# A hybrid decoder step on one core: TensorE's narrow matmuls, once grouped by head or by sampled token, taken in turn between column groups

## The reference, cut to what matters

```python
# stick-breaking attention, 8 heads of 64, prompt tokens among themselves
out = einsum("bhij,bjhd->bihd", weights, v)          # "value products" of the prompt
# the same for each sampled token over its 512 cached positions (4 pages of 128)
out = einsum("bhij,bjhd->bihd", weights, v_all)      # "value products" of the sampled tokens
# SSD (Mamba-2), 16 heads of 64, state 128, chunks of 128 tokens
y_diag = einsum("bclsg,bclsge,bcsgep->bclgep", cb, decay, xd)
y_off  = einsum("bclgn,bcgepn,bclge->bclgep", cc, h_in, exp(cs))
y = y_diag + y_off
```

## Time and profile before

| | |
|---|---|
| median of 3 runs | 1539.03 us (1538.46 to 1540.69) |
| profiled execution, span from first to last instruction | 1537.4 us (no other time is listed for it; 1.6 us lie between it and the median) |
| TensorE matmuls busy | 1486.9 us, 97% of the span |
| VectorE busy | 829.3 us, 54% |
| ScalarE busy | 496.8 us, 32% |
| GpSimd busy | 208.4 us, 14% |
| mean granted TensorE clock | 0.989 |
| attention turns | about 397 to 666 us |
| sampled tokens' values with their gate units | 773 to 849 us |
| SSD tiles | about 854 to 1002 us |

### The profile page before, as it was taken

How to read it: one execution, slowest core, us unless ns; L and a number is a source line. 1 busy time by engine, 2 the same in 40 slices (tenths; PEclk the granted TensorE clock), 3 DMA queues, 4 the chain that set the end, 5 groups by cost and what they waited for, 6 DMA issues and landing times.

```text
span 1537.4 us, 28766 instructions
## 1 busy us (share of the span) xinstructions
PE 1486.9 (97%) x11698; PEld 1425.1 (93%) x11698; DVE 829.3 (54%) x973; ACT 496.8 (32%) x715; POOL 208.4 (14%) x159
## 2 busy tenths in 40 slices
PE   5999999999999999996999998999999999999999
PEld 5999999999999898986976887889999999999999
DVE  6444444333364745676865699967554444443222
ACT  4222222222252433521222555454323222222121
POOL 4000000010000000033500567711020000000000
PEclk9999999999999999997999999999999999999999
DMA  5323323334331321354944835365523323323322
GB/s 154 97 82 95 95 83 92 97 102 121 96 90 55 89 82 55 95 201 142 318 142 130 124 112 157 77 183 172 165 82 97 95 82 95 95 83 89 100 89 79
DMA packets 279480, 172.56 MB, mean 112 GB/s; under 512 B 13344, under 2 KB 261376, under 8 KB 279296
## 3 DMA queue, kind: packets, MB, share of 16 engines
q1 hardware_dynamic: 273120, 156.80, 36.1%
q0 software_dynamic: 2848, 8.60, 1.7%
q10 hardware_dynamic: 3456, 6.39, 1.1%
HBM read 154.04 MB, written 17.73 MB: 112 GB/s over the span
## 4 chain that ended last, share of the span: by engine, by line
PE 86%; DVE 10%; DMA 2%; issue 1%; ACT 1%; SPq 1%; POOL 0%; DVEq 0%; ACTq 0%
PE ps L426 75%; PE ps L1802 3%; PE ps L1703 2%; DVE w_lo L407 2%; DVE gbuf L1260 2%; PE ps L1593 1%; PE ps L1619 1%; DVE bt L1101 1%; PE ps L1603 1%; DVE prod L1295 1%; PE ps L1609 1%; DMA out_ssd_p<-hin 1%; DVE hin L1253 1%; DVE ydec L1271 1%; PE ps L1583 0%
## 5 line engine op out<-in xcount | busy, mean ns | idle before, releaser
L426 PE MATMUL ps<-xg_hi,w_hi 128*128 128x260 f32 x2512 | 519.4, 288 | 37.2 <-DVE w_lo L407 32.0
L426 PE MATMUL ps<-xg_hi,w_lo 128*128 128x260 f32 x2512 | 510.7, 285 | 0.0
L426 PE MATMUL ps<-xg_lo,w_hi 128*128 128x260 f32 x2512 | 510.3, 285 | 0.0
L426 PEld LDWEIGHTS ps<-xg_hi,w_hi 128*128 128x128 f32 x2512 | 392.7, 191 | 49.7 <-issue 24.7
L407 DVE TENSOR_TENSOR w_lo<-stage,w_hi 128x1024 fp32r<-128x1024 f32 (+1 forms) x229 | 296.5, 1295 | 243.0 <-ACT w_hi L402 237.7
L426 PEld LDWEIGHTS ps<-xg_hi,w_lo 128*128 128x128 f32 x2512 | 392.2, 191 | 0.0
L426 PEld LDWEIGHTS ps<-xg_lo,w_hi 128*128 128x128 f32 x2512 | 391.6, 191 | 0.0
L402 ACT ACTIVATE w_hi<-stage 128x1024 fp32r<-128x1024 f32 (+1 forms) x229 | 237.1, 1035 | 316.2 <-PE ps L426 248.0
L426 PE MATMUL ps<-hid_hi,w_hi 128*128 128x260 f32 x704 | 141.9, 283 | 0.0
L426 PE MATMUL ps<-hid_hi,w_lo 128*128 128x260 f32 x704 | 141.5, 282 | 0.0
L426 PE MATMUL ps<-hid_lo,w_hi 128*128 128x260 f32 x704 | 141.3, 282 | 0.0
(11 more groups left out here) (282 smaller groups left out, 1598.5 us busy)
## 6 DMA issues: line engine op xcount, KB each, us to landing
stage<-in_w_in SPq DMA_DIRECT2D x69, 512.0 KB, 4.9
stage<-in_ffn_w_gate SPq DMA_DIRECT2D x44, 512.0 KB, 3.8
stage<-in_ffn_w_up SPq DMA_DIRECT2D x44, 512.0 KB, 3.9
stage<-in_ffn_w_down SPq DMA_DIRECT2D x32, 448.0 KB, 3.5
stage<-in_ffn_w_down SPq DMA_DIRECT2D x16, 512.0 KB, 3.7
pages<-in_cache_sb_k SPq DMA_DIRECT2D x32, 256.0 KB, 4.1
pages<-in_cache_sb_v SPq DMA_DIRECT2D x32, 256.0 KB, 3.2
gates<-gates_kept POOLq DMA_DIRECT2D x24, 260.0 KB, 3.6
```

The costliest lines, as they stand in the source:

```text
L426: mm = nc.tensor.matmul(out[:, h, :], wt[:, r, k, :], v[:, h * HALF:(h + 1) * HALF], start=start and k == 0 and n == 0, stop=stop and k == ...
```

## The change

In all three places the matmuls that write different rows of one PSUM bank, and so use different column groups of TensorE's array, are issued in turn. In attention both heads' value products stand together at the end of the turn. In the sampled part the four gate units of a turn come first and then the 16 matmuls of its four slots, page by page. In the SSD part `turn(t + 1)` moves ahead of both heads' products, `spread(t + 1, 0)` behind them, and the products wait for both heads' inputs; `turn` waits for ScalarE's two reads of bank 4 (`seg_ready`, `ecs_ready`) in place of the products made from them.

```diff
-                def values(e):
-                    pe.wait_ge(w_ready.sem, w_ready.now(t, e))
+                def values():
                     pe.wait_ge(v_tok_ready.sem, v_tok_ready.now(t))
-                    cols = slice(HD * e, HD * e + HD)
+                    pe.wait_ge(w_ready.sem, w_ready.now(t, 1))
                     for j in range(CH):
-                        mm = nc.tensor.matmul(ps[cols, 7, P * j:NP], v_tok[:, j, cols], ...
-                    mm.then_inc(pv_done.sem, 1)
+                        for e in range(2):
+                            cols = slice(HD * e, HD * e + HD)
+                            mm = nc.tensor.matmul(ps[cols, 7, P * j:NP], v_tok[:, j, cols], ...
+                            if j == CH - 1:
+                                mm.then_inc(pv_done.sem, 1)
...
                 unit(6)
-                values(0)
                 unit(7, end=2)
                 tails(1)
                 unit(7, begin=2)
-                values(1)
+                values()
...
                 for b in range(SLOTS):
                     gate(G0_V + b, SLOTS * i)
+                pe.wait_ge(wd4_ready.sem, wd4_ready.now(i))
+                for b in range(SLOTS):
                     pe.wait_ge(page_landed[b], 64 * i + 64 * (NS // SLOTS + 1))
-                    pe.wait_ge(wd4_ready.sem, wd4_ready.now(i))
-                    rows = slice(4 * SB_HEADS * b, 4 * SB_HEADS * (b + 1))
-                    for g in range(PAGES):
+                for g in range(PAGES):
+                    for b in range(SLOTS):
+                        rows = slice(4 * SB_HEADS * b, 4 * SB_HEADS * (b + 1))
                         mm = nc.tensor.matmul(ps[rows, 7, :], wd4[:, g, :],
                                               pages[:, b, g, :], start=g == 0, stop=g == PAGES - 1)
-                    mm.then_inc(pvd_done.sem, 1)
+                        if g == PAGES - 1:
+                            mm.then_inc(pvd_done.sem, 1)
...
             def turn(t):
                 pe.wait_ge(xs_ready.sem, xs_ready.now(t // SLOTS, t % SLOTS))
                 if t:
-                    pe.wait_ge(g_ready.sem, g_ready.now(0, 2 * t - 1))
-                    pe.wait_ge(csc_ready.sem, csc_ready.now(0, 2 * t - 1))
+                    pe.wait_ge(seg_ready.sem, seg_ready.now(0, 2 * t - 1))
+                    pe.wait_ge(ecs_ready.sem, ecs_ready.now(0, 2 * t - 1))
...
+                if t < SSD_T - 1:
+                    turn(t + 1)
                 for e in range(2):
                     pe.wait_ge(g_ready.sem, g_ready.now(0, 2 * t + e))
                     pe.wait_ge(csc_ready.sem, csc_ready.now(0, 2 * t + e))
-                    if e == 0:
-                        pe.wait_ge(hin_ready.sem, hin_ready.now(0, t))
-                        pe.wait_ge(y_ready.sem, y_ready.now(0, t - 1))
-                    rows = slice(HD * e, HD * e + HD)
-                    for c in range(CH):
-                        cols = slice(P * c, P * c + P)
+                pe.wait_ge(hin_ready.sem, hin_ready.now(0, t))
+                pe.wait_ge(y_ready.sem, y_ready.now(0, t - 1))
+                for c in range(CH):
+                    cols = slice(P * c, P * c + P)
+                    for e in range(2):
+                        rows = slice(HD * e, HD * e + HD)
                         nc.tensor.matmul(ps[rows, 7, cols], xd[:, t % 2, c, rows], gbuf[:, e, cols], start=True, stop=False)
+                    for e in range(2):
+                        rows = slice(HD * e, HD * e + HD)
                         mm = nc.tensor.matmul(ps[rows, 7, cols], hin[:, c, rows], csc[:, e, cols], start=False,
                                               stop=True)
-                    if e == 0 and t < SSD_T - 1:
-                        turn(t + 1)
-                        spread(t + 1, 0)
                 mm.then_inc(y_summed.sem, 1)
+                if t < SSD_T - 1:
+                    spread(t + 1, 0)
```

More of the change, by code:

```diff
@@ L1612, in tails @@
                     mm.then_inc(tail_summed.sem, 1)
-                def values(e):
-                    pe.wait_ge(w_ready.sem, w_ready.now(t, e))
+                def values():
                     pe.wait_ge(v_tok_ready.sem, v_tok_ready.now(t))
-                    cols = slice(HD * e, HD * e + HD)
+                    pe.wait_ge(w_ready.sem, w_ready.now(t, 1))
                     for j in range(CH):
-                        mm = nc.tensor.matmul(ps[cols, 7, P * j:NP], v_tok[:, j, cols],
-                                              zb[:, e, SCORE_AT[j]:SCORE_AT[j] + SCORE_W[j]],
-                                              start=j == 0, stop=j == CH - 1)
-                    mm.then_inc(pv_done.sem, 1)
+                        for e in range(2):
+                            cols = slice(HD * e, HD * e + HD)
+                            mm = nc.tensor.matmul(ps[cols, 7, P * j:NP], v_tok[:, j, cols],
+                                                  zb[:, e, SCORE_AT[j]:SCORE_AT[j] + SCORE_W[j]],
+                                                  start=j == 0, stop=j == CH - 1)
+                            if j == CH - 1:
+                                mm.then_inc(pv_done.sem, 1)
                 unit(0)
```

## The result

The changed kernel takes 1524.31 us (median of 4 runs, 1523.8 to 1526.46); the kernel before, beside it, 1538.74. The ratio is 0.9904, with a 95% interval of 0.9892 to 0.9916. By the medians that is 14.4 us less, by the ratio 14.8, where 12.9 had been forecast (1526 us; range 1519 to 1536). The profiled execution spans 1524.7 us, 12.7 less than the one before; it is the slowest of the four (1526.46 us), so its trace shows some 2 us less of the gain than the median does.

What follows compares the result with a forecast made beforehand. TensorE was taken to bound attention and the sampled part, VectorE the SSD tiles. The terms -6.4 - 7.1 + 0.6 = -12.9 us, from 1539.0, gave 1526 us, range 1519 to 1536.

Steps and rivals of the forecast that it cites:

- Two column groups run together: Narrow matmuls of two column groups, as in the last SSD tile, run at twice the rate of one.
- Four groups: Sampled tokens' value products: four column groups assumed to run all at once, 2 x 3.43 us for two blocks.
- rival of two streams: Sampled part: only two column groups overlap, L1703 at 7 us a block, gain there only -1.6 us.
- A, attention, -6.4 us: Four attention turns, both heads' value products merged: 2.25 us saved less 0.65 waited, 1.6 us per turn.
- B, sampled tokens, -7.1 us: Sampled part, two turns: 68.9 us against 76.0 with four streams, including a new wait and a lower clock.
- wait for the gate weights: Sampled part: TensorE stands 12.8 us, once, for gate weights queued behind SyncE's wait and sixteen page loads.
- lower clock: Sampled part: after the idle time TensorE resumes at granted clock 0.50, losing 2.4 us (bounds 0 and 3).
- C, SSD, +0.6 us: Eight SSD tiles: VectorE sets the pace, TensorE's savings become idle time; bounds -2 and +3 us.
- absorption of tile 0's 1.8 us by the store of `hin`: SSD tile 0: VectorE's 1.80 us wait for the output turns into a longer wait for the store of `hin`.
- dips of the clock: SSD: longer idle in front of tiles 2 and 4 slows the states product; two dips at 0.9 us, each as likely as not.
- faster SSD: Rival: SSD follows TensorE if VectorE's busy time is mostly contention shrinking with the new order; up to 14 us more, chance 0.06.
- rival without overlap: Column groups serialise: A +1.4, B +10.8, C +0.6, 1552 us; decided below about 1.4 matmuls in flight (44.6 / 31); chance 0.10.

Runs made afterwards that it cites:

- Experiment 4: Changed kernel with SyncE issuing the second turn's four gate loads and first short-convolution load ahead of its wait for slots: 1509.32 us, ratio 0.9808.
- Experiments 7 to 10: Kernel before, `gbuf` product on 128 of 512 columns, old/new SSD part: 1531.83/1531.75 us; sampled tokens' state work also cut to one token of eight: 1515.17/1503.17 us.
- experiment 8: Kernel before with only the SSD edit and VectorE's `gbuf` product on 128 of 512 columns, computation left out: 1531.75 us, ratio 0.9959.

## Why the prediction was right, step by step

**Two column groups run together.** Right: 16 records of two heads in 2.30 us, where I had 2.35.

**Four groups.** The open point of the prediction. All four run: a block takes 3.57 to 3.63 us in the chain, where I had 3.43 + 0.3. The rival of two streams (7 us a block) is excluded by 3.64 us. Beside it stood a rule of the Trainium skill (TensorE: Matmul & The Clock Gate, "The mechanism" in Part 3), that matmuls start and end strictly in program order. Between the column groups of this kernel the trace does not agree: in the earlier trace rows four records of L1773, 0.27 us or more each, lie within 0.44 us from 989.24, so the last has started by 989.41, although head 0's two records of L1774, the first at 989.45, stand ahead of head 1's in the program.

**A, attention, -6.4 us.** Measured -5.5 alone, -5.7 in the spans, and by the period of a turn 4 x 1.54 = -6.2, where I had 4 x 1.6. The wait for `spl_lo` came as reckoned, 0.41 us in front of the tails against 0.45, and a shorter one within them; the cover for the masked weights held.

**B, sampled tokens, -7.1 us.** Measured -7.7 alone, -8.2 in the spans. The wait for the gate weights was 11.9 us against 12.8; the landing took 4.3 in place of 5.1, which is most of the difference. The path was the forecast one, from the end of the block over SyncE's page loads to the landing, the rounding and the rest. The lower clock cost 25.46 - 23.24 = 2.2 us against 2.4. Experiment 4 shows the two to be 14 us, all of it the queue's: without it the part would have gained 22 us, and nearly two thirds of that were given back.

**C, SSD, +0.6 us.** Measured +0.8 alone, with an interval of -1.5 to +2.9, and +1.2 in the spans. The absorption of tile 0's 1.8 us by the store of `hin` came, whose wait grew from 1.99 to 3.65 us, and so did the dips of the clock: the states product takes 2.08 us in the even tiles 2, 4 and 6, where it was tile 6 alone before, and in tile 0 too. That the size fits is in part luck. Between the states products of tiles 1 and 7 the changed kernel takes 104.5 us against 105.7, and 107.1 with the SSD edit alone, so single traces scatter by more than the whole term. The loss that shows in the spans stands behind the last tile: from its states product to the end it is 563.5 us against 560.7, with a wait of 6.9 us for `w_lo` in place of 4.7, and the prediction has no term for that stretch.

The reason, too, was given too simply. I wrote that VectorE sets the pace, being 93% busy, and that a faster SSD would need its busy time to be mostly contention. It was in good part contention, only not one that the new order lessens. Experiments 7 to 10 correct this: VectorE's and GpSimd's work together hold the tiles above TensorE's pace, and with both lightened TensorE sets it. How the two share it is not shown, as said there.

**The rival without overlap.** Its price came out in no run, but one phrase is wrong: "31 us of savings needed" are not savings. The costs to be earned back are 1.4 + 10.8 + 0.6 = 12.8 us, and the 31 (44.6 - 12.8 = 31.8) are what the narrow work may still take; the 1.4 that follows is right.

**Sum.** Forecast 1526, measured 1524.3. Of the three parts none is off by more than 2 us, and the waits that A and B rest on came where they were expected.

## What to carry to other kernels

Narrow matmuls that use different column groups should be issued in turn, close to one another: side by side in blocks they overlap only at the borders. Before gathering work into one block, look at who waits for its first piece, and at what is queued behind that wait in its stream: here a freed buffer came later, and with it weights that had nothing to do with it (11.9 us, and 2.2 more at the lower clock). An engine that is busy all the time may be waiting within its instructions: compare the time of the same instruction where the engine beside it is quiet, here 1.23 us against 2.10, before calling it the limit.

## What the runs showed of the hardware that I had not expected

Four streams of 128x32 by 512 fp32 columns run at the rate of one each: 32 records in 3.64 us, against 13.7 in series. The overlap reaches about four records along the stream (an estimate from 4.9 us saved at three borders). A 128x128 product of VectorE took 1.25 us on average beside GpSimd's long products, and 0.41 us when those were cut to an eighth; a copy of ten columns took 1.8 us in experiment 8, against 0.16 before. Behind the 2.58 us of idle time in front of tile 2, in the windows of the changed kernel, the granted clock was 0.50, the 1.2 GHz level, and the states product took 2.08 us in place of 1.16:

```profile
872.60:875.20 2.60, 0.04 (x1) 0.00 (x0) 2.42 (x7) 0.61 (x2) 0.00 (x0) 1.00 0.88 262
875.40:882.10 6.70, 6.68 (x28) 5.96 (x28) 5.54 (x11) 5.74 (x17) 6.60 (x5) 0.50 0.43 130
```
